# First projection pair of three sub-layers fed from the residual before its norm, in a four-layer fp32 trunk

## What is computed

```
h = x * rsqrt(mean(x*x) + eps) * g          # rms_norm
h = h * (1 + scale) + shift                  # modulate, per channel
qkv = h @ w_qkv                              # moba: then rope on q and k
kv  = h @ w_kv                               # shared k (rope) and v of three branches
q   = h @ w_q                                # dilated mixer: rope on q
x = x + gate * y                             # after each sub-layer
```

## Time and profile before

| | us |
|---|---|
| median of 3 runs | 2489.45 (2488.74 to 2490.04) |
| the profiled execution | 2490.71 |
| its span, first to last instruction | 2489.0 |
| PE busy | 2443.6 (98%) |
| DVE busy | 1356.8 (55%) |
| ACT busy | 854.8 (34%) |
| POOL busy | 137.2 (6%) |
| mean granted clock of PE | 0.997 of full speed |

### The profile page before, as it was taken

One profiled execution on the slowest core, in us unless ns is written; L12 is line 12 of the kernel. 1 busy time (PEld: TensorE's weight loads), 2 busy tenths in 40 slices (PEclk: granted clock), 3 DMA queues, 4 the chain that ended last, 5 costly groups with the idle time before them and its releaser, 6 DMA issues. The chain is left out here.

```text
span 2489.0 us, 33283 instructions
## 1 busy us (share of the span) xinstructions
PE 2443.6 (98%) x11977; PEld 2015.8 (81%) x11985; DVE 1356.8 (55%) x2066; ACT 854.8 (34%) x1204; POOL 137.2 (6%) x128
## 2 busy tenths in 40 slices
PE   9999999999999999999999999999999999999998
PEld 6888886888778888878888888886888887888886
DVE  7555445677675654355545555445667667433333
ACT  3222223445443332233333333223344444333221
POOL 0000000112000000011211000000111110000000
PEclk9999999999999999999999999999999999999999
DMA  6666532665446654335557656345888973223332
GB/s 244 191 193 190 169 118 91 205 194 182 140 151 196 186 182 134 105 123 193 183 188 250 189 183 199 125 125 133 248 222 220 238 219 102 85 93 100 99 95 84
DMA packets 135714, 408.76 MB, mean 164 GB/s; under 512 B 17089, under 2 KB 17473, under 8 KB 135617
## 3 DMA queue, kind: packets, MB, share of 16 engines
q1 hardware_dynamic: 122560, 357.16, 47.6%
q0 software_dynamic: 13056, 50.33, 5.7%
HBM read 353.95 MB, written 52.43 MB: 163 GB/s over the span
## 5 line engine op out<-in xcount | busy, mean ns | idle before, releaser
L325 DVE TENSOR_TENSOR w_lo<-w_raw,w_hi 128x1024 fp32r<-128x1024 f32 (+2 forms) x386 | 473.3, 1227 | 650.5 <-ACT w_hi L321 650.5
L330 PE MATMUL ps<-h_hi,w_hi 128*128 128x512 f32 x1856 | 738.0, 398 | 11.0 <-DVE h_lo L880 4.6
L332 PE MATMUL ps<-h_hi,w_lo 128*128 128x512 f32 x1856 | 725.4, 391 | 0.0
L331 PE MATMUL ps<-h_lo,w_hi 128*128 128x512 f32 x1856 | 724.4, 390 | 0.0
L321 ACT CAST w_hi<-w_raw 128x1024 fp32r<-128x1024 f32 (+2 forms) x388 | 395.9, 1020 | 802.9 <-PE ps L332 788.2
L330 PEld LDWEIGHTS ps<-h_hi,w_hi 128*128 128x128 f32 x1856 | 349.6, 188 | 91.5 <-DVE h_lo L880 10.9
L332 PEld LDWEIGHTS ps<-h_hi,w_lo 128*128 128x128 f32 x1856 | 349.0, 188 | 74.2
L331 PEld LDWEIGHTS ps<-h_lo,w_hi 128*128 128x128 f32 x1856 | 349.9, 189 | 65.8
L330 PE MATMUL ps<-act_hi,w_hi 128*128 128x512 f32 x704 | 275.5, 391 | 0.0
L332 PE MATMUL ps<-act_hi,w_lo 128*128 128x512 f32 x704 | 274.2, 389 | 0.0
L331 PE MATMUL ps<-act_lo,w_hi 128*128 128x512 f32 x704 | 274.0, 389 | 0.0
(11 more groups left out here) (137 smaller groups left out, 2772.2 us busy)
## 6 DMA issues: line engine op xcount, KB each, us to landing
w_raw<-gate_up SPq DMA_DIRECT2D x176, 512.0 KB, 3.7
ada_raw<-ada SPq DMA_DIRECT2D x144, 512.0 KB, 4.6
w_raw<-down SPq DMA_DIRECT2D x80, 512.0 KB, 3.6
w_raw<-kv_w SPq DMA_DIRECT2D x48, 512.0 KB, 3.6
w_raw<-mixa_w SPq DMA_DIRECT2D x34, 512.0 KB, 4.3
w_raw<-mixb_w SPq DMA_DIRECT2D x34, 512.0 KB, 5.7
kb<-rot_st POOLq DMA_DIRECT2D x12, 1024.0 KB, 5.0
k_hi<-kb SPq DMA_DIRECT2D x64, 192.0 KB, 5.1
```

The source lines that it names most:

```text
L325: eng.tensor_tensor(w_lo[:, slot, 0:n], w_raw[:, slot, 0:n], w_hi[:, slot, 0:n].bitcast(F32), ALU.subtract).then_inc(w_lo_done[slot], 2)
L330: nc.tensor.matmul(out_ap, l_hi, r_hi, start=start, stop=False, skip_group_check=skip)
L331: nc.tensor.matmul(out_ap, l_hi, r_lo, start=False, stop=False, skip_group_check=skip)
L332: return nc.tensor.matmul(out_ap, l_lo, r_hi, start=False, stop=stop, skip_group_check=skip)
```

## The change

At the three borders behind ffn0, ffn1 and ffn2 the first pair (units 0 and 1) no longer multiplies h. During the down projection ACT and DVE make high and low parts of x * a for rows 0 to 5 as soon as x is updated, rows 6 and 7 after the root. PE multiplies them (`pe_late_pair`), with the square sum and the spreading of the factor between the rows, and sums shift @ w into four columns of bank 5, from the shift's high and low parts. DVE then adds these two parts (`late_scale`), multiplies the pair's banks by the factor into SBUF, and makes the cos and sin products from there with the shift added (`late_read`). The rows of h are made while the first pair runs, with the splits of units 2 and 3 between them, for pair 1 on. `mod_store` comes after unit 4's split. In mixB group 0 takes units 2 and 3 in the order 8, 9, 12, 13, 10, 11, 14, 15 of substeps, and its units use banks 0, 1, 2, 3, 1, 7 (before: 0, 1, 2, 0, 1, 2). SP issues unit 2 ahead of the tables. The border before ffn1, ffn3 and the final norm stay.

```diff
+LATE = ("mixA", "kv", "mixB")
+LATE_SPLIT = {"mixA": {1: 2, 5: 3}, "kv": {1: 2, 5: 3}, "mixB": {1: 2, 4: 3}}
+LATE_ROWS = (6, 7)
+FIRST_BANKS = (0, 1, 2, 3, 1, 7)
...
+        def pe_late_pair(pe, name):
...
+            def rows(ks, halves=(0, 1)):
+                for k in ks:
+                    pe.wait_ge(late_lo_done, KT * e + k + 1)
+                    for j in halves:
+                        mm = three_passes(ps[:, j, :], weights(w_hi, k, j), weights(w_lo, k, j),
+                                          h_hi[:, k, :], h_lo[:, k, :], k == 0, k == KT - 1)
...
+            def shift(ks, halves=(0, 1)):
+                for j in halves:
+                    for k in ks:
+                        for w in (w_hi, w_lo):
+                            mm = nc.tensor.matmul(shift_ps[:, 2 * j:2 * j + 2], weights(w, k, j), shift_hl[:, k, :],
...
+            if name == "mixB":
+                rows(range(4), (0,))
+                sums()
+                rows((4, 5), (0,))
+                pe.wait_ge(w_lo_done[1], u0 + 2)
+                rows((0, 1), (1,))
+                spread()
+                rows((6, 7), (0,))
+                shift(range(KT), (0,))
+                rows(range(2, KT), (1,))
+                shift(range(KT), (1,))
+            else:
+                rows((0, 1))
+                sums()
+                rows((2, 3))
+                spread()
+                shift(range(4))
+                pe.wait_ge(w_lo_done[1], u0 + 2)
+                rows(range(4, KT))
+                shift(range(4, KT))
+            pe.sem_inc(shift_summed, 1)
...
+            pe.wait_ge(pair_free, p0 + 2)
+            pe_pair(pe, u0 + 2, p0 - 1, 2, FULL_KS, kv_h_hi, kv_h_lo, h_ready)
+            pe.wait_ge(shift_done, LATE.index("kv") + 1)
+            pe.wait_ge(mod_ready, ADA_IN_FFN[1] + ADA_LOOPED + 1)
+            values(0)
...
+        def late_scale(dve, name):
...
+            dve.wait_ge(shift_summed, e + 1)
+            nc.vector.tensor_reduce(shift_out[:], shift_ps.rearrange("p (j h) -> p j h", j=2),
+                                    mybir.AxisListType.X, ALU.add).then_inc(shift_done, 1)
+            dve.wait_ge(unit_used, UNIT0[name] + 2)
+            dve.wait_ge(rb_kept_done, e + 1)
+            view = by_class if name == "mixA" else classes
+            for j in range(2):
+                nc.vector.tensor_tensor(view(scaled[:, j, :]), classes(ps[:, j, :]), classes(factor),
+                                        ALU.mult).then_inc(late_scaled, 1)
...
+                op = nc.vector.scalar_tensor_tensor(out=tmp[:, n, :], in0=scaled[:, src, :],
+                                                    scalar=shift_out[:, src:src + 1], in1=table[:],
+                                                    op0=ALU.add, op1=ALU.mult)
...
+                if name in LATE and name != "kv":
+                    act.wait_ge(late_used, KT * LATE.index(name) + k + 1)
...
+            if name in LATE:
+                act.wait_ge(xar_done, x0 + KT)
+                nc.scalar.copy(late_views(name)[0], rb).then_inc(rb_kept_done, 1)
+                w_split_hi(act, UNIT0[name] + 4, 0)
...
-            for j in range(2):
-                w_dma(sp, u0 + j, j, weights[j])
+            for j in range(3):
+                w_dma(sp, u0 + j, j % 2, weights[j])
             load_tables(sp, name)
-            for j in (2, 3):
-                w_dma(sp, u0 + j, j % 2, weights[j])
+            w_dma(sp, u0 + 3, 1, weights[3])
...
                         if pair == 0:
-                            split(2)
-                        split(2 * pair + 3)
+                            late_read(dve, name, rope0, 0)
+                            split(4)
+                            late_read(dve, name, rope0, 1)
+                            mod_store(dve, stored)
+                            split(5)
+                            rot_low(dve, rot_n(g, 0))
+                            continue
+                        if pair == 2:
+                            split(7)
                         read_out(g, pair, 0)
                         read_out(g, pair, 1)
...
-            act_norm(act, "mixA", SUB_BLOCK[1])
...
+            for n in LATE_ROWS:
+                late_high(act, "mixA", n, 2)
+            act_norm(act, "mixA", SUB_BLOCK[1])
```

More of the change, by code:

```diff
@@ L596, in substep @@
                 unit = n // 4
+                first = isinstance(g, int) and g == 0
+                follows = first and n < 2 * KT
                 if n % 4 == 0:
@@ L611, in substep @@
                     if n % 4 == 0:
-                        pe.wait_ge(pair_free, g * 3 + p0 + pair + (1 if unit in (0, 2, 4) else 2))
+                        pe.wait_ge(pair_free, g * 3 + p0 + pair + (1 if unit in (0, 2, 4) or first else 2))
+                        if first and unit == 5:
+                            pe.wait_ge(mod_ready, ADA_BLOCKS)
                     for j in range(2):
@@ new lines, in dve_norm @@
+        def dve_norm(dve, name, r, block, gain_row, col_n):
+            h0, view = h_count(name), by_class if name == "mixA" else classes
+            to_hi, to_lo = (kv_h_hi, kv_h_lo) if name == "kv" else (h_hi, h_lo)
+            if name not in LATE:
+                dve.wait_ge(mod_ready, block + 2)
+                nc.vector.scalar_tensor_tensor(out=a_col[:], in0=mod[:, block + 1, :], scalar=1.0,
+                                               in1=gain[:, gain_row, :], op0=ALU.add,
+                                               op1=ALU.mult).then_inc(col_ready, 1)
@@ L1052, in body @@
                         w_split_hi(act, u + n_u + 1, (n_u - 1) % 2, split_sizes(ks, n_u - 1))
-            loop_of_two(act, body, name == "ffn3")
+                    if late is not None:
+                        for j in range(2):
+                            if i * 4 + 2 * b + j not in LATE_ROWS:
+                                late_high(act, late[0], i * 4 + 2 * b + j, late[1])
+            loop_of_two(act, body, name == "ffn3", late is not None)
         def loop_of_two(eng, body, last, unrolled=False):
@@ L1068, in dve_residual @@
             dve.wait_ge(col_ready, col_n)
+            if late is not None:
+                late_cols(dve, *late, col_n + 1)
             def body(i, last):
@@ L1759, in read_out @@
                 else:
-                    rope_multiply(dve, 2 * pair % 3, (2 * pair + 1) % 3, g * 6 + rope0 + 2 * pair, (half,))
+                    banks = 2 * pair % 3, (2 * pair + 1) % 3
+                    if isinstance(g, int) and g == 0:
+                        banks = FIRST_BANKS[2 * pair:2 * pair + 2]
+                    rope_multiply(dve, *banks, g * 6 + rope0 + 2 * pair, (half,))
             def rot_n(g, pair):
```

215 lines of the change are left out of this document (157 added, 58 removed).

## The result

The changed kernel takes 2505.28 us (median of 4 runs, 2503.87 to 2505.89) where the kernel before takes 2489.66 beside it: ratio 1.0062, interval [1.0045, 1.008]. The forecast was 2476.7, faster by 12.7 us; it is slower by 15.6. The profiled execution took 2505.76 for a span of 2504.0, against 2489.0 for the span of before.

A forecast was written before the change was run, and what follows sets the result against it. TensorE was taken as the bound, 98% busy, with VectorE setting the pace at the borders. Gains 2.2 (mixA) + 4.3 (kv) + 6.2 (mixB) = 12.7 us off 2489.45 gave 2476.7; own range 2474 to 2479.5, wider 2472 to 2482.

The forecast's parts named there:

- The columns of 128x8 ... I cost at nothing.: The short column instructions and peeled loop bodies were priced at nothing, as hidden behind the same products.
- Border mixB, gain 6.2: At the second mixer's border, unit 4's split and the k burst come sooner, so unit 7 starts earlier: gain 6.2 us.
- the burst keeps its length, so that point comes 6.2 earlier: At mixB, with an unchanged k load burst, TensorE begins unit 7 at 1755.9 instead of 1762.10.
- Border mixA, gain 2.2: At the first mixer's border, VectorE's chain and k's landing limit the gain to 2.2 us, not pair 1's 7.6.
- Border kv, gain 4.3: At the kv border, the second pair begins at 1088.6 instead of 1092.91, without idle: gain 4.3 us.
- The shift matmuls, 0.115: At each border, 32 added two-column matmuls cost 0.115 us each, 3.7 in all; bounds 0.06 and 0.45 each.
- the rivals on dear matmuls: Two-column matmuls at 0.25 us each: gain 4.1, 2485.4, chance 0.06; at 0.45: slower by 13.4, 2502.9, chance 0.03.
- The factor 1.35 later: At mixA, the factor reaches VectorE 1.35 us later after the transposes' start, at 413.05 instead of 411.70.
- the clock falls: Small matmuls and unfilled waits lower the clock, costing 1.6 to 2 us each at kv and mixB: 2480.3, chance 0.15.
- here only the start does: Against the clock rival: in the kernel before, only the start shows throttling, not mixA and mixB.
- The rival on the losing side: Two-column matmuls at 0.45 us each make the kernel slower by 13.4 us, 2502.9; chance 0.03.

The follow-up runs named there:

- the kernel with 160 bytes: The changed kernel with 160 unused bytes behind the shift tensors, putting the stage buffers 256 bytes above their place before: 2485.36 us, ratio 0.9976.
- The last run: Fillers in the four longest new waits, added to the 2481.3 us kernel (160 bytes, head 1's k loaded ahead of `load_q`): 2477.29 us, ratio 0.9949.
- the run with the loads last: The kernel with 160 bytes, with the second mixer's k and v loads for head 1 issued behind `load_q` at group 0's end: 2482.86 us, ratio 0.9973.

## Why the prediction was wrong

- **"The columns of 128x8 ... I cost at nothing."** This is the step that failed, by 20.4 us. The new instructions did cost nothing, and no stage is missing time for them. Their storage did cost: 96 bytes ahead of the stage buffers, which slow the down projections by 12.6 us and kv's products by 7.8, stages and products that the forecast took to stay as they were. With the storage put right (the kernel with 160 bytes) the change gains 4.5 us of the forecast 12.7, so this step alone doesn't account for the miss; the next one does for most of the rest. Every edit had a price for its time on an engine and none for the place that it takes.
- **Border mixB, gain 6.2.** The first half held. Pair 1 ends 28.4 us behind the transposes' start (forecast 28.5), and SP passes unit 6 at 29.2 where it did at 34.7. The step that failed is "the burst keeps its length, so that point comes 6.2 earlier". Before, the first store of rotated q was issued 1.5 us behind the first k load, and ScalarE waited 0.9 for POOL alone; now it comes 5.2 behind, with all eight loads, unit 7 and a load of v ahead of it. The burst came 5.4 earlier, the store only 1.7. A wait of 7.24 stands where 3.4 was forecast, and a low clock behind it. With the wait for unit 7 the first score is 0.35 earlier than before, of 6.2; the attention steps behind it then take 341.3 us for 339.2, with a lower clock at 2024 to 2032, which makes the loss of 1.7. (In the kernel with 160 bytes, where the clock doesn't fall there, they take 339.3.)
- **Border mixA, gain 2.2.** Right: 2.34 at the first score, 2.07 at the stage's end. The wait for unit 4 was 2.08 (2.9), the one before the score 3.60 (3.1). Its reason was only half right: what binds between the late read-out and k's landing runs through POOL and ScalarE, and `mod_store` has room beside it.
- **Border kv, gain 4.3.** Right: 4.7. The second pair starts 17.1 us behind the transposes' start where it started 21.8 behind, with no idle time; with 160 bytes the stage as a whole is 4.6 shorter.
- **The shift matmuls, 0.115.** They start 0.111 apart; bounds of 0.06 and 0.45 were far off on both sides, and the rivals on dear matmuls fall. By the figure of 81 ns (the Trainium skill, "TensorE: Matmul & The Clock Gate", section "Back-to-back issue gap") 16 of them would by estimate take 1.3 us; they take 1.8.
- **The factor 1.35 later.** 1.07 (8.42 for 7.35 behind the transposes' start).
- **The rival "the clock falls"**, 0.15, came true in other places. Behind the stretches of shift matmuls the windows show 1.00. It fell at the end of the wait of 3.60 (0.57 in the window behind it) and late in the one of 7.24 (0.50). The forecast held that the waits absorb a fall; what of a fall lies behind a wait isn't absorbed by it. The Trainium skill (same page, section "HAM oscillation — how this bites in real kernels") says that waits between bursts throttle the array anew. The last run agrees at three of its four places, where the clock had fallen and stays at 1.00 with fillers. Against this rule the forecast held that "here only the start does". That reading of the kernel before missed a fall, in mixA's attention behind a wait of 2.33 us:

```profile
632.00:636.00 4.00, 4.00 (x12) 2.84 (x11) 2.48 (x6) 2.33 (x5) 0.00 (x0) 0.57 0.46 130
```

- **How sure the fall is.** It isn't certain behind a short wait: behind 2.08 in the changed kernel the clock stayed at 1.00, behind 2.14 in the run with the loads last it fell:

```profile
434.00:436.00 2.00, 1.66 (x9) 1.66 (x10) 2.00 (x3) 0.00 (x0) 1.42 (x1) 0.66 0.33 84
436.00:438.00 2.00, 2.00 (x11) 2.00 (x11) 1.97 (x4) 0.00 (x0) 1.27 (x1) 0.50 0.46 178
```

- **The rival on the losing side** was dear matmuls, 0.03. The true one, a stage that the change doesn't touch, was in no case, so the range could not hold the result.

What stays open: why the distance matters, and to which neighbour. The runs moved the operand that isn't the weights (`act_hi` and `act_lo`, or `kv_h_hi` and `kv_h_lo`) against `w_hi`, `w_lo` and everything else below at once, so the weights are the likely partner and not shown to be. That a multiple of 256 bytes is fast rests on 0 and +256; +32, +64, +96 and +128 are slow by unequal amounts. Nor was it shown what drops the clock at 2024 to 2032, where the kernel before has the same wait of 1.48 us and keeps 1.00, nor how much of the differences of 1 to 4 us between the last kernels is spread from run to run.

## What to carry to other kernels

When a change adds a tensor, list the places of all buffers behind it before and after, and look first at the spacing of products in a stage that the change doesn't touch; padding the distance back to its old multiple cost nothing here and was worth 20 us. Where a stage starts sooner, ask for each buffer that exists once what its release is queued behind, and follow the whole chain of stores, since moving a burst off one put it on the next. When a wait moves, ask whether the fillers that covered it should move along; before a gain is put down to them, look for the place in the timeline where it arises.

## What the runs showed of the hardware

The spacing of three-pass products with both operands in SBUF depends on the distance of the buffers. Here `act_hi` and `kv_h_hi` are moved from their old places; the means are over all four down projections, and over kv behind its first pair:

| moved by, bytes | down projections, us | kv, us |
|---|---|---|
| 0 | 0.2282 | 0.2268 |
| 32 | 0.2339 | 0.2334 |
| 64 | 0.2300 | 0.2325 |
| 96 (the change) | 0.2341 | 0.2339 |
| 128 | 0.2336 | 0.2324 |
| 256 | 0.2281 | 0.2269 |
| all by 128 | 0.2281 | 0.2268 |

A store of rotated rows that followed eight loads of k, a unit of weights and a load of v kept its buffer for 12.3 us, for at most 8.0 where it followed only the first of the loads. POOL's add of 128x512 took 1.27 us beside VectorE's reduce from PSUM and 2.20 beside its split of weights in SBUF.
